# Chunked RWKV-7 recurrence: every product on a 64x64 quarter of the array, and the tiles interleaved in ten half levels

## The reference, cut to what matters

```
def step(S, inp):
    r_t, w_t, k_t, v_t, a_t, b_t = inp
    sa = jnp.einsum('bhij,bhj->bhi', S, a_t)
    S = S * w_t[:, :, None, :] + sa[..., None] * b_t[:, :, None, :] + v_t[..., None] * k_t[:, :, None, :]
    y = jnp.einsum('bhij,bhj->bhi', S, r_t)
    return S, y
```

## Time and profile before

| | |
|---|---|
| median of 3 runs | 3053.22 us (3052.01 to 3053.93) |
| the profiled execution, its time | 3051.1 us |
| its span, first to last instruction | 3049.3 us |
| mean granted clock of TensorE in it | 0.947 |
| PE busy, share of the span | 91% |

### The profile page before, as it was taken

The page is one execution under the profiler, slowest core; times in us unless marked ns, Lnnn a source line. Parts: engine busy times, 40 slices in busy tenths (PEclk is TensorE's granted clock), DMA queues, the critical chain, the costliest instruction groups (busy, mean ns, idle before and its releaser), DMA issues. The chain is left out here.

```text
span 3049.3 us, 45421 instructions
## 1 busy us (share of the span) xinstructions
PE 2783.7 (91%) x18805; PEld 2294.4 (75%) x18805; DVE 1259.2 (41%) x2065; ACT 775.4 (25%) x1469; POOL 305.5 (10%) x256
## 2 busy tenths in 40 slices
PE   9799999999977998979999999996989987999866
PEld 8799999999856655758888888875768844888555
DVE  6333333333342466343333333335243334554546
ACT  6211111111151188232111111112111122222221
POOL 1100000000030044120000000005000001222102
PEclk9899999999988999989999999998999986999978
DMA  3211111111036400321111111113012100000032
GB/s 140 76 50 55 41 41 41 61 43 42 29 126 150 148 2 29 104 104 56 42 54 49 41 62 41 42 65 136 28 35 83 48 6 6 3 3 3 3 117 97
DMA packets 57934, 175.51 MB, mean 58 GB/s; under 512 B 7742, under 2 KB 15455, under 8 KB 56624
## 3 DMA queue, kind: packets, MB, share of 16 engines
q1 hardware_dynamic: 57778, 173.27, 17.1%
HBM read 146.30 MB, written 26.36 MB: 57 GB/s over the span
## 5 line engine op out<-in xcount | busy, mean ns | idle before, releaser
L769 PE MATMUL f0gu<-b1XH,f0w0H 128*128 128x346 f32 (+1 forms) x528 | 170.3, 323 | 12.6 <-DVE f0w0L L697 12.6
L723 DVE TENSOR_TENSOR Y<-f0dn,Y 128x512 f32<-128x512 f32 (+1 forms) x180 | 124.0, 689 | 113.6 <-PE f0dn L793 112.6
L712 DVE TENSOR_TENSOR f1hf<-f1sg,f1gu 128x512 f32<-128x512 f32 x44 | 30.3, 688 | 340.2 <-ACT f1sg L665 340.2
L771 PE MATMUL f0gu<-b1XH,f0w0L 128*128 128x346 f32 (+1 forms) x528 | 170.4, 323 | 0.0
L712 DVE TENSOR_TENSOR f0hf<-f0sg,f0gu 128x346 f32<-128x346 f32 (+1 forms) x66 | 34.1, 517 | 329.1 <-ACT f0sg L665 329.1
L770 PE MATMUL f0gu<-b1XL,f0w0H 128*128 128x346 f32 (+1 forms) x528 | 169.7, 321 | 0.0
L771 PE MATMUL f0gu<-b1XH,f0w1L 128*128 128x346 f32 (+1 forms) x528 | 169.7, 321 | 0.0
L769 PE MATMUL f0gu<-b1XH,f0w1H 128*128 128x346 f32 (+1 forms) x528 | 169.4, 321 | 0.0
L770 PE MATMUL f0gu<-b1XL,f0w1H 128*128 128x346 f32 (+1 forms) x528 | 169.0, 320 | 0.0
L769 PE MATMUL f1gu<-b1XH,f1w0H 128*128 128x512 f32 x352 | 139.0, 395 | 11.9 <-DVE f1w0L L697 11.9
L723 DVE TENSOR_TENSOR Y<-f1dn,Y 128x512 f32<-128x512 f32 x160 | 109.2, 690 | 90.6 <-PE f1dn L793 90.6
(11 more groups left out here) (392 smaller groups left out, 6516.3 us busy)
## 6 DMA issues: line engine op xcount, KB each, us to landing
f0raw<-in_w_gate_up SPq DMA_DIRECT2D x44, 512.0 KB, 5.3
f1raw<-in_w_gate_up SPq DMA_DIRECT2D x44, 512.0 KB, 5.2
residual<-Y SPq DMA_DIRECT2D x32, 512.0 KB, 2.8
Y<-in_w_ada SPq DMA_DIRECT2D x8, 1536.0 KB, 6.3
f0rawd<-in_w_down SPq DMA_DIRECT2D x22, 512.0 KB, 3.6
f1rawd<-in_w_down SPq DMA_DIRECT2D x22, 512.0 KB, 3.6
w_in_b_raw<-in_w_in_b SPq DMA_DIRECT2D x17, 512.0 KB, 3.7
w_in_a_raw<-in_w_in SPq DMA_DIRECT2D x12, 512.0 KB, 4.1
```

Of the source, the lines that this page charges most:

```text
L712: dve.tensor_tensor(hf[:, i, 0:w], sg[:, i, 0:w], gu[:, i, 1, 0:w], ALU.mult).then_inc(s["mul"], 1)
L723: dve.tensor_tensor(y, dn[0:r, (par * ND + i) % 4], y, ALU.add).then_inc(s["acc"], 1)
L769: pe.matmul(o, wH[c][:, j, k], xh, start=(k == 0), stop=False)
L771: last = pe.matmul(o, wL[c][:, j, k], xh, start=False, stop=(k == KC - 1))
```

## The change

The stage is written anew with the same mathematics, chunk and number of levels.

- Token-indexed operands of the heads e = 1 lie on the partitions of the other chunk: `at(e, q)` is q for e = 0 and 1 - q for e = 1. Products of the two heads and two chunks then go to the quarters (0,0), (0,1), (1,0) and (1,1).
- S is compact: 64 columns for a pair instead of 128. The transposes are products with a 64x64 identity. The decay sums are eight products on 64 rows each. The products of kk with ab are computed a second time for e = 1, in the plain place.
- The halves of a level are pairs of c (g = 0, 1) instead of e. There are ten halves h. PE's order in half h is: product(h), then pieces of the chain of tile t - 1 and of the preparation of tile t + 1, then update(h - 1). DVE's is: the add of h - 1 (`added`), then its pieces. XX, LT have two copies, the token-indexed tiles three.
- POOL makes Uo for both halves of a level in one instruction of 128x512, and adds the identity for the whole tile in one.
- The masks are loaded twice side by side in two loads, where there were two loads.

The lines added, cut to their core (the lines removed are those of `recurrence_stage` printed above; the helpers for views are cut):

```diff
--- before.py
+++ after.py
+        def at(e, q):
+            return rows(q if e == 0 else 1 - q)
...
+        def XT(t, e, c, q):
+            return XX[at(e, q), t % 2, c // 2, 1 + e, H * (c % 2):H * (c % 2 + 1)]
+        def Xi(t, e, c, q):
+            return XX[rows(q), t % 2, c // 2, 3 * e, H * (c % 2):H * (c % 2 + 1)]
...
+                def other(t, l):
+                    da.wait(pool, t, "lt")
+                    if l >= 3:
+                        pp.wait(pool, t, f"p{2 * (l - 3) + 1}")
+                    else:
+                        pp.wait(pool, t - 1, f"p{2 * (l + LV - 4) + 1}")
+                    po.mark(pool.tensor_tensor(Uo[:, slot(t, l)], LT[:, t % 2], wide(lvl[l]), ALU.mult), f"u{l}")
+                def start(t):
+                    da.wait(pool, t, "xm")
+                    pi.mark(pool.tensor_tensor(turned(t), turned(t), wide(eye), ALU.add), "eye")
+                    other(t, 1)
+                start(0)
                 for t in range(NT):
...
+                def added(t, h):
+                    g = h % 2
+                    px.wait(dve, t, f"x{h}")
+                    lo, hi = (1, 3) if h // 2 == LV - 2 else (0, 4)
+                    x = XX[:, t % 2, g, lo:hi].rearrange("p s x -> p (s x)")
+                    dl.mark(dve.tensor_tensor(x, x, inv[:, g].rearrange("p e x -> p (e x)")[:, P * (1 + lo):P * (1 + hi)], ALU.add), f"a{h}")
+                def applied(t, q):
+                    pd.wait(dve, t, f"sa{q}")
+                    aw.wait(dve, t, "uu")
+                    pd.wait(dve, t - 1, "y1")
+                    for e in range(2):
+                        o, x = at(e, q), slice(4 * H * e, 4 * H * (e + 1))
+                        dd.mark(dve.tensor_tensor(SA[o, x], ch[o, x], UU[o, x], ALU.add), f"sa{q}{e}")
+                def stepped(t, q):
+                    pd.wait(dve, t, f"st{q}")
+                    pd.wait(dve, t, "ys1" if q else "ys0")
+                    dd.mark(dve.tensor_tensor(Sx[:, :, :], S[:, :, :], ch[:, 0:4 * H].rearrange("p (c t) -> p c t", c=4), ALU.add), f"sx{q}")
+                    dd.wait(dve, t, f"sx{q}")
+                    d = ein[:, t % 3, :, H * q + H - 1:H * q + H].broadcast_to([P, 4, H])
+                    dd.mark(dve.tensor_tensor(S[:, :, :], Sx[:, :, :], d, ALU.mult), f"s{q}")
...
+                for t in range(NT + 1):
+                    more = t + 1 < NT
+                    for h in halves:
+                        if h >= 1 and t < NT:
+                            added(t, h - 1)
+                        if h == 0:
+                            if t:
+                                added(t - 1, HL - 1)
+                            if more:
+                                decayed(t + 1, "at")
+                        if h == 1 and more:
+                            decayed(t + 1, "bt")
+                        if h == 2 and more:
+                            decayed(t + 1, "kt")
+                        if h == 3:
+                            if t:
+                                applied(t - 1, 0)
+                            if more:
+                                masked(t + 1)
+                        if h == 4 and t:
+                            stepped(t - 1, 0)
+                            reads(t - 1)
+                        if h == 5:
+                            if t:
+                                applied(t - 1, 1)
+                            if more:
+                                decayed(t + 1, "rt")
+                        if h == 6 and more:
+                            keys(t + 1)
+                        if h == 7 and t:
+                            stepped(t - 1, 1)
             @block.tensor
             def _(pe):
...
+                def cum(t):
+                    if t:
+                        aa.wait(pe, t - 1, "tkv")
                     for c in range(4):
                         for q in range(2):
+                            mm = pe.matmul(wk[:, q, P * c:P * (c + 1)], lw[rows(q), t, P * c:P * (c + 1)], tris[rows(q)].rearrange("p a t -> p (a t)"), start=True, stop=True)
+                    pa.mark(mm, "cum")
...
+                def inner(t):
+                    da.wait(pe, t, "bt")
+                    if t >= 2:
+                        aw.wait(pe, t - 2, "wt")
+                    else:
+                        aa.wait(pe, t, "ein")
+                    for c in range(4):
+                        for q in range(2):
+                            for e in range(2):
+                                gram(ab, kk, t, e, c, q, at(e, q), 0)
+                            mm = gram(ab, kk, t, 1, c, q, rows(q), 1)
+                    pa.mark(mm, "ab")
...
+                def inverse_start(t):
+                    pi.wait(pe, t, "eye")
+                    da.wait(pe, t, "ak")
+                    for c in range(4):
...
+                                mm = pe.matmul(wk[rows(q), e, o:o + H], XT(t, e, c, q), cst[at(e, q), 1, 0], start=True, stop=True)
+                    pa.mark(mm, "tx")
...
+                def turn(t, pair, n):
+                    aa.wait(pe, t, "xi" if n == "tab" else "tab")
+                    da.wait(pe, t, "kt")
+                    for c in range(4):
+                        for i, src in enumerate(pair):
+                            for q in range(2):
+                                for e in range(2):
+                                    mm = pe.matmul(wk[at(e, q), e, 4 * H * i + H * c:4 * H * i + H * (c + 1)], src[rows(e), c, chunk(t, q)], b.ident[rows(e), rows(e)], start=True, stop=True)
+                    pa.mark(mm, n)
...
+                def product(t, h):
+                    l, g = 1 + h // 2, h % 2
+                    po.wait(pe, t, f"u{l}")
+                    if h >= 2:
+                        dl.wait(pe, t, f"a{h - 2}")
+                    else:
+                        aa.wait(pe, t, "xi")
+                        dl.wait(pe, t - 1, f"a{h + HL - 2}")
+                    for cc in range(2):
+                        c, o = 2 * g + cc, slice(H * cc, H * (cc + 1))
+                        for q in range(2):
+                            for e in range(2):
+                                mm = pe.matmul(inv[at(e, q), g, e, P * e + H * cc:P * e + H * (cc + 1)], Uo[rows(q), slot(t, l), g, e, o], Xi(t, e, c, q), start=True, stop=True)
+                    pp.mark(mm, f"p{h}")
+                def update(t, h):
+                    l, g = 1 + h // 2, h % 2
+                    al.wait(pe, t, f"m{h}")
+                    for cc in range(2):
+                        c, o = 2 * g + cc, slice(H * cc, H * (cc + 1))
+                        if l < LV - 1:
+                            for q in range(2):
+                                for e in range(2):
+                                    x0 = 0 if e else P
+                                    pe.matmul(inv[rows(q), g, e, x0 + H * cc:x0 + H * (cc + 1)], XT(t, e, c, q), mid[at(e, q), g, e, o], start=True, stop=True)
+                        for q, e in ((0, 0), (1, 0), (1, 1), (0, 1)):
+                            mm = pe.matmul(inv[at(e, q), g, 0, (2 + e) * P + H * cc:(2 + e) * P + H * (cc + 1)], mid[at(e, q), g, e, o], XT(t, e, c, q), start=True, stop=True)
+                    px.mark(mm, f"x{h}")
...
+                def values(t):
+                    da.wait(pe, t, "ak")
+                    aa.wait(pe, t, "tkv")
+                    if t:
+                        dd.wait(pe, t - 1, "rk")
+                    else:
+                        da.wait(pe, t + 1, "xm")
...
+                                mm = pe.matmul(wk[at(e, q), 0, head(e, c)], AK[at(e, q), head(e, c)], T[at(e, q), t % 3, 3, head(e, c)], start=True, stop=True)
+                    pm.mark(mm, "mv")
...
+                def closed(t):
+                    dl.wait(pe, t, f"a{HL - 1}")
+                    if t + 2 < NT:
+                        aa.wait(pe, t + 2, "ein")
...
+                    for c in range(4):
+                        for q in range(2):
+                            for e in range(2):
+                                mm = pe.matmul(wk[rows(e), q, H * c:H * (c + 1)], T[at(e, q), t % 3, 0, head(e, c)], XT(t, e, c, q), start=True, stop=True)
+                    pw.mark(mm, "wt")
+                    am.wait(pe, t, "mv")
+                    dd.wait(pe, t - 1, "sx1")
+                    for c in range(4):
+                        for q in range(2):
+                            for e in range(2):
+                                mm = pe.matmul(ch[at(e, q), head(e, c)], XT(t, e, c, q), MV[at(e, q), head(e, c)], start=True, stop=True)
+                    pw.mark(mm, "uu")
...
+                def chain(t, n):
+                    q = int(n[-1]) if n[-1] in "01" else 0
+                    if n in ("ys0", "ys1"):
                         if q:
+                            dd.wait(pe, t, "s0")
                         else:
+                            ad.wait(pe, t - 1, "y")
+                            dd.wait(pe, t - 1, "s1")
```

(98 more changed lines are left out.)

438 lines of the change are left out of this document (178 added, 260 removed).

## The result

The changed kernel takes 3075.16 us (median of 4 runs, 3069.19 to 3079.54) against 3052.72 beside it (4 runs, 3052.01 to 3053.93): ratio 1.0065, 95% interval 1.0053 to 1.0078. It is slower, by some 22 us, where I had forecast 3.6. A second session gave 3083.58 (4 runs, 3074.68 to 3085.68), ratio 1.0089, 1.0073 to 1.0105. The traced execution took 3069.19 us, 18.1 more than the one of before (17.6 by their spans).

What follows compares the result with a forecast made beforehand. PE's issue bounds the old stage; the new tile's 22.7 issue, 0.3 shape changes, 10.3 open adds and 2.15 chain waits make 35.4 us for 35.9. With the ends, the stage grows 3.6 us: 3056.8 us, range 3030 to 3100.

Steps and rivals of the forecast that it cites:

- rival A: Whole kernel: the forecast's own sum holds, 3056.8 us, own range 3045 to 3069; chance 0.45.
- Steps 1 to 5: PE's issue per tile: quarter products cut it by 8.5 us to 22.7, with changes of shape 0.3 us for 2.1.
- rival B: Two-quarter groups: neighbours on different quarters overlap, 22 ns a record for 29, 23 us saved, 3034 us; chance 0.22.
- rival C: Four-quarter groups: 15 ns does not hold, 22 ns a record, 35 us more, 3092 us; chance 0.15.
- Step 6: Between update(h-1) and product(h+1): PE waits for DVE's add ten times a tile, 1.08 or 0.81 us each, 10.3 us.
- the bound of 0.8: PE's idle before a product: under 0.8 us would make the forecast wrong in kind.
- Step 7: Chain of tile t - 1: PE's waits for SA, reads, S, rk and sx1 sum to 2.15 us a tile; POOL and ACT hidden.
- Step 8: Stage's ends: first product after 16.7 us, tile 0 29 us partly at half clock, tile 7 29.2, then 13.4.
- 6 x 35.4: The six steady tiles of the stage: 35.4 us each, for 35.9 before.
- rival D: PE's clock: idle over 1 us a half keeps or brings it to 0.50 past tile 0; 45 us, 3102 us; chance 0.14.

Runs made afterwards that it cites:

- experiment 1: The changed kernel with update(h - 1) moved right behind product(h), ahead of the chain and preparation pieces: 3038.30 us, ratio to before 0.9937.
- experiment 2: An unused DVE operation of the same size ahead of each add: 3124.65 us in the changed kernel, 3053.22 us in that of experiment 1.
- experiment 4: experiment 1 with added products ahead of the updates of levels 1 to 4: 3093.89 us 64 columns wide, 3065.87 us in half as many of 128.
- experiment 5: experiment 1 with unused 128x512 products in TensorE's prologue waits: 3041.88 us with eight in the first wait, 3041.26 us with four.

## Why the prediction was right, and where it was short

The mechanism was right as far as it went: PE's issue fell, the open add took it back, and the kernel came out slower, within the range. The size was short: 22 us for 3.6, of which the stage has 10.9. Both medians, 3075 and 3084, lie above rival A's own range of 3045 to 3069; that they lie in the whole range owes to its width of 70 us, made for rivals that did not come true as described, and is luck as far as the number goes.

- **Steps 1 to 5, PE's issue of 22.7 us a tile.** The prices hold as prices: L2109's 32 records in 0.68 us and L2068's 16 in 0.46 are 15 ns, L2116's 29 in 1.03 are 29. Groups on two quarters go at 27 to 30 ns, so rival B's 22 is nowhere; nor is rival C's 22 for four quarters, outside pauses and stretches of half clock: it was 15 ns in every ordinary half, also in groups of 64. The Trainium skill, "TensorE: Matmul & The Clock Gate", section "Wait — 56ns, not 53.3ns?", says that start to start is never below about 25 ns; the 15 ns of this trace differ from it, and the measurement decides.
- **Step 6, the open add.** 1.08 us from issue to issue: measured 2621.53 less 2620.43 (the last update record's bar of 0.22 ends at 2620.65), 1.10. 72 waits for the add of 60.7 us in all are 0.84 each behind the last bar, just above the bound of 0.8 that I had set, and experiments 1 and 2 show from both sides that it sets the tile. DVE's add of 128x512 took 0.69 us here as before, while the group of products ahead of it fell from 29 to 15 ns a record. The Trainium skill, "TensorEngine Tiling (Array Packing)", PSUM Bottleneck, says that tiling does not speed up PSUM's evacuation; this trace agrees.
- **Step 7, chain waits.** 2.15 us a tile forecast; the rows for SA, S, the reads and rk sum to some 0.8. Too high by 1.3 us. The tile of 35.2 to 35.4 came out as summed since another wait, put down to ACT (6 times 0.6 us), and, by the difference, some 0.8 us more of issue than my 22.7 made up for it; that the two errors cancelled is luck. POOL's 128x512 took 1.28 us and ACT's copy of 1,024 elements 1.02, hidden as said.
- **Step 8, the ends.** First product 16.4 us after the start (16.7), tile 0 29.4 (29), from the start of tile 7 on 42.0 (42.6).
- **The term that failed: "6 x 35.4".** The six tiles took 220.2 us, not 212.4: 7.8 more, where the whole stage missed by 7.3. The sum knew PE, the other engines and the clock, but not where the instructions come from. The change adds 1,856 matmul records and as many loads to the page's PE line, all in this stage; the queue had to bring 36 packets for 29 in the same 160 us. At 8.3 packets a tile and 3.8 us each the supply needs 31.5 us of the 35.4: enough on the mean, too slow for halves that issue 64 records at 15 ns in a row. The pauses, 6.6 us in that trace and 9.2 in the second, and the clock behind some of them are the rest. By the sign that I had set for rival D, a clock of 0.50 past tile 0, D came true in part: it had the fall within a tile ("in halves 4 and 5"), but from idle that adds up and not from a late packet, and its 45 us stand against at most 6.8 that four stretches of 3.4 us at half clock can cost.
- The 6.7 us outside the stage are not explained. The medians differ from before by 22 and 28 us in two sessions, and the traced execution of each was its fastest run; that others have more pauses, as the second trace has (its six tiles took 223.7 us for 220.2), is likely but shown for these two only.

## What to carry to other kernels

A product cut into quarters gives back time only if what comes between two dependent products still covers the other engine's step. Put the update right behind the product and the pieces behind the update; here that one move was worth 37 us and turned a loss of 0.65% into a gain of 0.6%. Before counting on 15 ns a record, count the instructions: divide the stage's load and matmul records (an f32 product has two of each) by 256, multiply by 3.8 us, as measured in this kernel, and compare with the time the stage would take. Where the two come near, wider moving operands with the same columns are the cheaper form, but not stationary blocks that leave half of the rows unused.

## What the runs showed of the hardware that was not expected

TensorE's instructions come in packets of 16 KB, 256 of them by the counts. In experiments 1, 4 and 5 the packets started not closer than 3.3 us and 3.8 to 4.0 us apart on the mean: some 15 ns an instruction, 30 ns for a load with its product, twice the 15 ns of a quarter group. A pause stands at the border of a packet and ends 1.2 to 1.9 us behind the end of one. The same 2,112 instructions of a tile took 35 us where PE waited for DVE in every half and 31.5 where the supply was left, with one open add. And a stop of a microsecond in the supply could bring the granted clock from 1.00 to 0.50 for 3.4 us soon behind it, so that it was paid twice. It did not always: stops of 0.91 us in the first trace and of 1.66 and 1.62 in the second had no fall behind them, and what decides is open.
